# HGRN2 level and diagonal scores as two 64-column products per chunk, with the levels in neighbouring pairs

## The reference

```python
G = jnp.cumsum(gc, axis=2)
diff = jnp.where(causal[:, :, None], G[:, :, :, None, :] - G[:, :, None, :, :], -jnp.inf)
attn = jnp.einsum('bhtk,bhsk,bhtsk->bhts', qc, kc, jnp.exp(diff))
o = jnp.einsum('bhts,bhsv->bhtv', attn, vc) + jnp.einsum('bhtk,bhkv->bhtv', qc * jnp.exp(G), state)
```

## Time and profile before

| what | us |
|---|---|
| median of 3 runs | 1311.4 (1308.51 to 1311.83) |
| the profiled execution: its time | 1311.31 |
| its span, first to last instruction | 1309.5 |
| PE busy | 1214.9 (93%) |
| POOL busy | 617.4 (47%) |
| DVE busy | 752.3 (57%) |
| ACT busy | 441.6 (34%) |
| mean granted TensorE clock | 0.976 |

### The profile page before, as it was taken

The page is one execution under the profiler, slowest core; times in us unless marked ns, Lnnn a source line. Parts: engine busy times, 40 slices in busy tenths (PEclk is TensorE's granted clock), DMA queues, the critical chain, the costliest instruction groups (busy, mean ns, idle before and its releaser), DMA issues.

```text
span 1309.5 us, 30234 instructions
## 1 busy us (share of the span) xinstructions
PE 1214.9 (93%) x11354; PEld 996.4 (76%) x11354; DVE 752.3 (57%) x1343; ACT 441.6 (34%) x835; POOL 617.4 (47%) x584
## 2 busy tenths in 40 slices
PE   2999999999999999999997889999699999989995
PEld 1778878878788788787886768878477777768873
DVE  6545474475465655754745341176746866868447
ACT  4342242242332422423334231032525242543123
POOL 3643441442433414423333127778365664747771
PEclk9999999999999999999999879999799999999997
DMA  5221120221111212202112023333122222322331
GB/s 206 81 59 42 54 62 26 65 59 34 54 46 50 59 27 67 64 26 59 49 43 72 17 90 97 112 89 97 49 81 81 73 81 67 85 64 72 98 89 65
DMA packets 46723, 88.66 MB, mean 68 GB/s; under 512 B 5808, under 2 KB 6832, under 8 KB 46384
## 3 DMA queue, kind: packets, MB, share of 16 engines
q1 hardware_dynamic: 44352, 82.70, 21.5%
q10 hardware_dynamic: 2288, 4.72, 1.1%
HBM read 85.30 MB, written 2.10 MB: 67 GB/s over the span
## 4 chain that ended last, share of the span: by engine, by line
PE 78%; DVE 14%; ACT 4%; issue 3%; DMA 1%; SPq 0%; DVEq 0%; ACTq 0%
PE psum L320 76%; DVE mix L1344 3%; ACT mix L931 3%; DVE mix L1368 2%; PE psum L868 1%; DVE mix L1872 1%; DVE h_split L1348 1%; DVE mix L1790 1%; DVE mix L1801 1%; DVE mix L1864 1%; DVE mix L1855 1%; PE psum L440 1%; DVE mix L1870 1%; DVE y L1876 1%; DMA mix<-xT 1%
## 5 line engine op out<-in xcount | busy, mean ns | idle before, releaser
L320 PE MATMUL psum<-h_split,w_hi 128*128 128x512 f32 x2320 | 750.9, 405 | 29.1 <-DVE mix L1445 11.1
L320 PEld LDWEIGHTS psum<-h_split,w_hi 128*128 128x128 f32 x2320 | 429.2, 191 | 137.2 <-issue 42.2
L303 POOL TENSOR_SCALAR w_hi<-w_raw 128x512 fp32r<-128x512 f32 x290 | 208.3, 718 | 641.9 <-PE psum L320 506.4
L320 PE MATMUL psum<-h_split,w_lo 128*128 128x512 f32 x1160 | 457.3, 394 | 0.0
L305 POOL TENSOR_TENSOR w_lo<-w_raw,w_hi 128x512 fp32r<-128x512 f32 x290 | 409.6, 1412 | 24.2
L320 PE MATMUL psum<-mix 64*64 64x64 f32 (+5 forms) x7552 | 346.0, 239 | 18.0 <-DVE mix L1496 7.4
L320 PEld LDWEIGHTS psum<-mix 64*64 64x64 f32 (+3 forms) x7552 | 312.4, 142 | 63.3 <-issue 34.2
L931 ACT ACTIVATE mix<-psum 128x512 f32<-128x512 f32 (+4 forms) x292 | 136.9, 489 | 473.6 <-PE psum L320 339.8
L320 PEld LDWEIGHTS psum<-h_split,w_lo 128*128 128x128 f32 x1160 | 220.7, 190 | 48.4
L931 ACT ACTIVATE mix<-mix 128x512 f32<-128x512 f32 (+2 forms) x274 | 142.0, 551 | 170.3 <-DVE mix L1773 71.2
L1438 DVE COPY_PREDICATED mix<-mask,psum 128x128 f32<-128x128 uint8 (+2 forms) x272 | 108.8, 440 | 106.0 <-PE psum L320 92.7
(11 more groups left out here) (113 smaller groups left out, 620.8 us busy)
## 6 DMA issues: line engine op xcount, KB each, us to landing
w_raw<-wall SPq DMA_DIRECT2D x290, 256.0 KB, 2.6
mix<-xT SPq DMA_DIRECT2D x4, 512.0 KB, 5.2
mix<-mask_f SPq DMA_DIRECT2D x1, 2048.0 KB, 11.8
mix<-xT ACTq DMA_DIRECT2D x1, 2048.0 KB, 7.9
out<-mix SPq DMA_DIRECT2D x8, 256.0 KB, 2.1
mix<-pT ACTq DMA_DIRECT2D x2, 512.0 KB, 4.0
mix<-lru_w ACTq DMA_DIRECT2D x4, 256.0 KB, 3.4
mix<-w2a ACTq DMA_DIRECT2D x16, 32.0 KB, 2.0
```

The source lines that it names most:

```text
L303: pool.tensor_scalar(w_hi[:, slot, :, :], w_raw[:, slot, :], 1.0, 0.0, ALU.mult, ALU.add).then_inc(sem["w_hi"], 1)
L320: return pe.matmul(o, lhsT, rhs, start=start, stop=stop, skip_group_check=True)
```

## The change

Levels 0 to 5 and the diagonal compute, per chunk, only the two quadrants in which query and key lie in the same half of 64 tokens (the masks of these levels and of the diagonal lie within them): one product of 64 keys by 64 queries on the array's lower 64 columns and one on its upper 64 columns. Banks 4 and 5 are cleared once at the start, so that the masked copies read no undefined quadrant. In PE's order each of the last two hops (5 and 6) is followed by a quarter of tile 5; levels 0 and 1 come together after it, directly ahead of `state_outputs`; tile 6 runs in one piece, with levels 4 and 5 together behind it. On DVE `hop_state(r, 6)` comes before `masked(0)`.

```diff
@@ hg_level, hg_diagonal
                 for c in range(CH):
-                    at = slice(c * L, (c + 1) * L)
+                    even, odd = slice(c * L, c * L + 64), slice(c * L + 64, (c + 1) * L)
                     if lvl < LEVELS - 1:
-                        last = mm(o[:, at], keys[:, at], qp[:, lvl % 4, at])
+                        mm(o[0:64, even], keys[:, even], qp[:, lvl % 4, even])
+                        last = mm(o[64:P, odd], keys[:, odd], qp[:, lvl % 4, odd])
                     else:
-                        even, odd = slice(c * L, c * L + 64), slice(c * L + 64, (c + 1) * L)
                         last = mm(o[0:64, odd], keys[:, even], qp[:, lvl % 4, odd])
...
                 for c in range(CH):
-                    last = mm(H1[:, c * L:(c + 1) * L], hk[:, c * L:(c + 1) * L], hq[:, c * L:(c + 1) * L])
+                    even, odd = slice(c * L, c * L + 64), slice(c * L + 64, (c + 1) * L)
+                    mm(H1[0:64, even], hk[:, even], hq[:, even])
+                    last = mm(H1[64:P, odd], hk[:, odd], hq[:, odd])
@@ even_round of PE
                 if pair:
                     hop(r, 5)
-                level(0)
+                t(5, 0, 2)
                 if pair:
                     hop(r, 6)
+                t(5, 2, 4)
+                level(0)
                 level(1)
-                t(5, 0, 4)
                 if pair:
                     state_outputs(r)
                 if head:
...
                 t(5, 4, KC)
                 level(2)
                 level(3)
-                t(6, 0, 4)
+                t(6)
                 level(4)
-                t(6, 4, KC)
                 level(5)
@@ start of DVE
             dve.memset(attn, 0.0)
+            dve.memset(psum[:, 4:6, :], 0.0)
@@ even_round of DVE
                     hop_add(r, 6)
+                    hop_state(r, 6)
                     between(masked, 0)
-                    hop_state(r, 6)
```

## The result

| | before | after |
|---|---|---|
| median, us | 1311.62 (4 runs, 1308.51 to 1313.85) | 1298.11 (4 runs, 1296.13 to 1299.25) |
| profiled execution | 1311.31 | 1298.86 |
| span | 1309.5 | 1297.1 |

The account below looks back on a forecast made before the run. PE's stream was taken as the bound: 2.07 us a round (0.52 + 0.52 + 0.68 + 0.35), 14.5 over rounds 1 to 7, plus 1.3 in round 0; 1311.4 - 15.8 = 1295.6 us, range 1291.5 to 1301.5.

Parts of the forecast that it names:

- What bounds: PE's stream between hop 5 and tile 7 sets the round; PE busy 585.8 of 595.0 us in nearly rounds 1 to 7.
- rival of POOL or DVE taking it all: POOL's weights or DVE's work take up the whole gain, leaving 1311.4 us; chance 3%.
- The price of a pair: In the new levels, two 64-column products side by side take 0.058 us a pair; bounds 0.058 to 0.11.
- The slower rival: In every new level and the diagonal, pairs don't pair: 0.11 us each, 23.3 us more, 1318.9; chance 4%.
- Entries, exits and the change from 128x64 to 64x64 tiles: Around PE's tiled blocks: entry 0.32 us plus 0.05, exit to projection products 0.72, shape change 0.20 (bounds 0.06 and 0.20).
- Blocks of 1.96 and 3.32: Levels 2, 3 and levels 4, 5 take 1.96 us each; levels 0, 1 with `state_outputs` and `hg_values` 3.32.
- `hg_keys` behind DVE's copy of level 6: After the diagonal, `hg_keys` waits for DVE's copy, 0.06 us from copy to PE; block 2.36, gain 0.35.
- Spare time ahead of `hg_values`: Level 0's masked copy is ready 0.34 us before PE needs it; in round 0 PE waits 0.62.
- Hops 5, 6 ...: each hop as hop 4 now: Hops 5 and 6 take 0.93 us each; with levels 0, 1, `state_outputs` and `hg_values` the gain is 0.68 a round.
- the second rival: New PE wait, at `hg_values` or level 6's copy, 0.3 to 1.0 us a round: 1298 to 1303.6; chance 12%.

Follow-up runs that it names:

- early_gate: Changed kernel with DVE's product that gates tile 3 and frees bank 1 moved to right behind the second hop's sum: 1294.04 us, ratio to before 0.9858.
- before_gate: Kernel before the change, with DVE's product that gates tile 3 moved to right behind the second hop's sum: 1310.62 us, ratio to before 0.9989.
- order_only: Changed kernel's order on PE and DVE, but levels 0 to 5 and the diagonal as one 128x128 product per chunk: 1314.34 us, ratio to before 1.0021.
- tile_by_tile: Changed kernel with each level's and the diagonal's four lower-column products first, then the four upper, instead of in turn: 1306.67 us.
- levels_apart: Changed kernel with level 4 back between the halves of tile 6 and level 5 behind it: 1299.12 us, beside the changed kernel's 1298.37.
- tiles_only: Kernel before with the two 64-column products per chunk and the cleared banks, in the old order: 1299.44 us, ratio to before 0.9901.

## Why the prediction was right, and where its sum was off

- **What bounds:** right. PE's stream from hop 5 to tile 7 got shorter and the rounds with it; no rival of POOL or DVE taking it all came out.
- **The price of a pair:** right. The 32 records of two levels take 1.15 with the last 0.22, so 0.93 for 15 steps and the first 0.05: 0.058. The slower rival (0.11, loads one after the other) is out.
- **Entries, exits and the change from 128x64 to 64x64 tiles:** right. Blocks of 1.96 and 3.32 came out at 1.96, 1.97 and 3.33, the last only with the 0.20 for the new change of shape. The Trainium skill (TensorEngine Tiling, Key Properties) says that a change of tiling mode drains the engine. The trace agrees: at this change 0.15 us pass from start to start and the first step is 0.05 longer, where two pairs within a shape are 0.058 apart.
- **`hg_keys` behind DVE's copy of level 6:** right in kind, 0.06 short (2.42 for 2.36): `hg_keys` starts 0.14 after the copy's end (338.54 - 338.40), not 0.06.
- **Spare time ahead of `hg_values`:** there in rounds 1 to 7, gone in round 0, as forecast.
- **The step that failed:** "Hops 5, 6 ...: each hop as hop 4 now". It priced hop 5 with a projection piece behind it by hop 4's row, but behind hop 4 comes tile 4 (bank 0, long free), behind hop 5 tile 5 (bank 1, which DVE frees only behind its fifth hop sum). In the kernel before only hops 1 to 4 had a quarter of tile 4 behind them; hop 5, which the words on that kernel count with them, was followed by level 0, which needs another bank. The prediction listed the waits of the steps that moved later and left out what a step needs that moved earlier: `t(5, 0, 2)` was to come forward by 2.0 us, from 2.15 behind hop 5 to 0.14. It is the second rival, a new wait of 0.3 to 1.0 a round, at another place than named: 0.43 a round, 3.0 us. The run `early_gate` takes it away and comes out at 1294.0, 1.6 below the forecast for the change; of its 4.1 us less, 3.0 lie in these rounds.
- **The rest of the account, and luck:** with 0.43 and 0.06 less, and small differences of 0.01 to 0.02 elsewhere, a round gains 1.58 by the rows of round 3. In the traces rounds 1 to 7 outside the inverse sections gain 10.9 and the blocks of round 0 another 1.3, together 12.2. The profiled spans say 12.4, the medians 13.5. The spans agree only because three stretches without any change nearly cancel: 0.9 was lost ahead of the first projection product (below), 1.4 behind the even rounds, which was not followed up, and 2.6 was won in the inverse sections (167.2 before, 164.6 after). So that the measured gain comes as near to 15.8 as 13.5 is partly luck: the steps that the forecast added up gave 12.2. Part of the 2.6 are pauses in which PE waited for nothing that the profile shows; in the kernel before, rounds 1 to 7:

```profile
PE psum L320 <- issue: 2.4, 4, 0.8
```

  After it is 1.3 (above), and in the eight other profiles 0.3 to 1.4. `before_gate` took 166.0 in the inverse sections, the changed kernel run again 163.1 and `order_only`, which has no tiles, 164.2. So the tiles don't explain it, and two profiles of one kernel differ by 1.6 there; what these pauses wait for stays open and wasn't tried.

## What to carry to other kernels

When a piece of work is moved ahead, list what it needs (its bank, its buffer, its inputs) and who delivers each, and when; not only who waits for what moved back. Products on column tiles pay in blocks: here two levels together gained 0.51 and one alone 0.08, since entering and leaving cost as much as a level saves. Before filling a standing wait, ask how much slack the next engine's chain has behind it.

## What the runs showed of the hardware that was not expected

- Neighbouring products on one column tile still overlap partly with those of the other tile behind them: 22 steps for 32 records in `tile_by_tile`.
- The start. DVE's seven sums of squares took 7.88 us before and 8.91 after, and the first projection product came 0.9 later:

```profile
11.32 8.91 DVE L1370 TENSOR_TENSOR mix<-mix 128x512 f32<-128x512 f32 x7 [2.33 <-DMA mix<-xT]
```

  The fill of the banks alone doesn't bring this: DVE was idle for 2.33 ahead of the first sum, and four of the eight profiles with the fill, those of `order_only` and `levels_apart` among them, show 7.88. The other four show 8.9, and the two profiles without the fill (before and `before_gate`) 7.88, so that the fill has no part in it is not shown. The length of one such sum goes from 0.69 to 1.57 (before: minimum 0.69, median 0.91, maximum 1.57) while POOL splits the first weights, so it may depend on how the two fall on each other; that was read from the timeline and not tried. In `tiles_only` the sums took 7.88 but began 0.9 later, after a longer wait for x (3.37), with the same late first projection product.
